# Hybrid layer with experts: the state-space branch product as plain block products between queries and keys, with resident left operands

## The chip, the cores and the metric

The program runs on one core of a Trainium2 chip. The metric is the device time of one execution in microseconds (us); of several runs the median is given. TensorE (PE) multiplies, VectorE (DVE) and ScalarE (ACT) work element by element, GpSimd (POOL) too, and SyncE (SP) issues most of the transfers (DMA), in order.

## The reference, cut to what matters

A layer of two blocks on 1024 tokens with 1024 features, in float32. The change touches only the first block:

```python
h = _rmsnorm(x, pre_g)
proj = jnp.einsum('bld,de->ble', h, w_in)
z_ssm, xbc, dt_raw, q, k, v, f_raw, z_att, g_ssm, g_att = jnp.split(proj, ...)
xbc = jax.nn.silu(_causal_dwconv(xbc, conv_w, conv_b))
...
y_ssm = ...            # y * silu(z_ssm), normed by groups, times a gain
o = _forgetting_attention(heads(q), heads(k), heads(v), log_f)
y_att = o * jax.nn.silu(z_att)
p_ssm = jnp.einsum('ble,ed->bld', y_ssm, w_branch_ssm)
p_att = jnp.einsum('ble,ed->bld', y_att, w_branch_att)
merged = jax.nn.sigmoid(g_ssm) * p_ssm + jax.nn.sigmoid(g_att) * p_att
out = jnp.einsum('bld,de->ble', merged, w_out)
```

## The kernel before

Every large product is made of three matmuls on rounded operands: each float32 operand is split into a high part (rounded, by ACT) and a low part (the rest, by DVE), and PE adds high*high, high*low and low*high.

**The xbc phase** (`phase_dense`, "xbc") multiplies h by the columns of xbc and one half of g_ssm: 5 jobs of 8 steps of 24 matmuls, with the causal convolution (`convolve_xbc`) and the decays (`Decays`) on DVE beside it, 6 taps of the convolution in step 8. `KeptOperands` (L1064) meanwhile writes the operands of the later products of h to DRAM (`h_ops`): the split quarters A11 to A22 in steps 0 to 7 (L1086), and four sums S1 to S4 of each of 4 chunks, which POOL adds (L1127 to L1132), ACT rounds (L1110) and POOL splits (L1141).

**`phase_units`** (L1247) computes z, the other half of g_ssm, the queries, keys and values of the attention, and the branch product of y. A unit is a product of 1024 tokens by 1024 columns. A "full" unit uses Winograd's form of Strassen's scheme: 7 products of half-size blocks (`FULL`), whose left operands A and S come from DRAM and whose right operands are sums of quarters of the weights, made by DVE in place (L1500 to L1506). A "half" unit (512 columns) has 4 plain products (`HALF`). A product takes 4 steps; a step multiplies one left by one right operand of 128 rows in 12 matmuls (L1413 to L1416). There are 39 products, 156 steps: z (steps 0 to 27), half of g_ssm (28 to 43), queries (44 to 71), keys (72 to 99), values (100 to 127), branch product (128 to 155).

Left operands (512 KB, high and low) come to four places `bs_a` (L1322), each free when the step 4 earlier is multiplied. Right operands are rounded by ACT (L1432) and split by DVE (L1511) into three places `bs_b`. When a product ends, ACT evicts it (`take`, L1446) or DVE joins it to an earlier one (`join`, L1524), from PSUM to SBUF. For queries, keys and values ACT and DVE then split the result (`finish`, L1471 and L1535), and SP stores the high and the low part, 1 MB each (L1340, L1341), four such pairs a unit. The order of each engine's work is written out by step: at step n an engine first does the step's own operand, then `take` and `join` of product step n-2, `finish` of n-3, and what `beside` and `aside` hang in. SP at n loads the left operand of n, weights that fall due (`load_later`), stores of the product that ended at n-5, and what `on_queue` gives it.

`GatedTurn` (L1557) multiplies y by silu(z), norms and transposes it into yT, PE's part of it before step 44. The operands of the branch product are made of yT by `MadeOperands` (L1145) at every second step from 48 on: 28 operands (7 of each of 4 chunks), of which POOL adds the sums, ACT rounds (L1183) and DVE splits (L1191) into two places `mo_s`, and which SP stores to `y_ops` (L1199) four steps later. Before rounding into a place ACT waits for that place's store:

```python
            if x >= self.RING:
                act.wait_ge(self.kept[x % self.RING], 16 * (x // self.RING))
```

The branch product is the last unit; POOL multiplies it by the gate (L1369). `on_queue` fetches the first heads of the attention at step 138. `phase_forget_attention` (L1719) follows: PE multiplies heads for the row maxima (L1858), DVE takes them (L2029), PE transposes them (L1878), ACT copies them (L1986), sends them to DRAM and fetches them back as a row (L1991, L1996), and then PE scores (L1896). `tail.stored` (L1241) lets an engine wait for all stores of queries, keys and values.

## Time and profile before

| | us |
|---|---|
| median of 3 runs | 2961.45 (2961.43 to 2963.57) |
| the profiled execution | 2964.42 |
| its span, first to last instruction | 2962.6 |
| `phase_units`, first to last product | 524.73 |
| PE busy, share of the span | 93% |
| mean granted clock of PE | 0.964 of full |

The page gives busy times by engine and the costliest groups; the trace behind it answers for a stretch, a line or a tile. A granted clock of 1.00 is 2.4 GHz, 0.50 is 1.2 GHz. Matmuls are pipelined, so the distance between the starts of two is the cost of one, not the time in which one is busy.

### The profile page before, as it was taken

Reading aid. Unit: us, or ns where it says so; the run is one execution under the profiler, and the core shown is the slowest. Engines: PE = TensorE matmul, PEld = TensorE weight load, DVE = VectorE, ACT = ScalarE, POOL = GpSimd, SP = SyncE. Lnnn points to the kernel's source line nnn. Section 1 sums busy time; section 2 is a strip of 40 time slices with the busy share of each in tenths; the row PEclk is TensorE's granted clock in tenths of the full one; section 3 lists DMA queues with packets and bytes.
Section 4 is the critical chain, followed back from the end, with each engine's and each line's share of the span. In section 5 each row is a group of like instructions: output and inputs, shape, how many; then the busy total and the mean of one; then the engine's idle time right before and its main releaser. Section 6 shows DMA issues by size and latency. Waiting matters only on the chain.

```text
span 2962.6 us, 36347 instructions
## 1 busy us (share of the span) xinstructions
PE 2747.2 (93%) x13166; PEld 2244.2 (76%) x13166; DVE 1984.7 (67%) x2312; ACT 1465.7 (49%) x2232; POOL 618.5 (21%) x458
## 2 busy tenths in 40 slices
PE   7899989877888999999998998899999899999997
PEld 6687978766766777788787886778778788888876
DVE  5876756655545555343643687799773699988886
ACT  4544436433323666434343256733432277777775
POOL 3300500100004777100100000000010034333332
PEclk9999989988998999999999998999999999999999
DMA  7420057699886665213212110011213599999996
GB/s 219 169 78 21 1 205 279 229 336 328 283 291 173 138 148 117 61 50 106 84 49 63 50 43 1 15 43 50 100 39 135 186 379 383 370 366 366 367 355 204
DMA packets 199982, 509.61 MB, mean 172 GB/s; under 512 B 75649, under 2 KB 75777, under 8 KB 175008
## 3 DMA queue, kind: packets, MB, share of 16 engines
q1 hardware_dynamic: 189296, 490.78, 48.6%
q0 software_dynamic: 9216, 16.81, 2.3%
q8 instruction: 89, 1.46, 0.2%
q14 instruction: 53, 0.43, 0.0%
q10 hardware_dynamic: 1328, 0.14, 0.0%
HBM read 433.91 MB, written 90.51 MB: 177 GB/s over the span
## 4 chain that ended last, share of the span: by engine, by line
PE 46%; DMA 17%; DVE 9%; POOL 5%; issue 5%; ACT 4%; SPq 1%; POOLq 0%; DVEq 0%; ACTq 0%; PEldq 0%
DMA ex_raw<-in_w_down_e 8%; PE ps L901 7%; PE ps L902 7%; PE ps L903 7%; POOL fa_pl L1841 5%; PE ps L1413 3%; PE ps L1415 3%; PE ps L1416 3%; DMA y_ops<-mo_s 3%; DVE ex_w L3637 3%; PE ps L3487 2%; DMA ex_raw<-in_w_up_e 2%; ACT ex_w L3572 2%; DMA bs_a<-h_ops 1%; PE ps L3215 1%
## 5 line engine op out<-in xcount | busy, mean ns | idle before, releaser
L3637 DVE TENSOR_TENSOR ex_w<-ex_raw,ex_w 128x2048 fp32r<-128x2048 f32 x190 | 430.6, 2289 | 63.8 <-ACT ex_w L3572 61.5
L3572 ACT ACTIVATE ex_w<-ex_raw 128x2048 fp32r<-128x2048 f32 x190 | 361.8, 1917 | 112.4 <-DMA ex_raw<-in_w_up_e 55.0
L3487 PE MATMUL ps<-ex_w,ex_xT 128*128 128x512 f32 x1536 | 367.3, 395 | 14.5 <-DVE ex_xT L3652 14.4
L3487 PEld LDWEIGHTS ps<-ex_w,ex_xT 128*128 128x128 f32 x1536 | 286.5, 189 | 80.1 <-issue 15.6
L1511 DVE TENSOR_TENSOR bs_b<-arena,bs_b 128x512 fp32r<-128x512 f32 x156 | 116.3, 751 | 153.2 <-ACT bs_b L1432 152.9
L793 DVE SCALAR_TENSOR_TENSOR arena<-arena,small 128x1023 f32<-128x1023 f32 (+9 forms) x168 | 215.4, 1282 | 3.5
L1841 POOL TENSOR_TENSOR fa_pl<-fa_p,fa_ph 128x512 fp32r<-128x512 f32 x192 | 196.3, 1039 | 81.4 <-ACT fa_ph L1979 79.3
L1413 PE MATMUL ps<-bs_a,bs_b 128*128 128x512 f32 x400 | 163.7, 409 | 45.0 <-DVE arena L1524 14.5
L1432 ACT ACTIVATE bs_b<-arena 128x512 fp32r<-128x512 f32 x156 | 96.7, 629 | 197.9 <-PE ps L1416 173.3
L3487 PE MATMUL ps<-ex_w,ex_hT 128*128 128x512 f32 x768 | 182.8, 393 | 0.3 <-issue 0.2
L3487 PEld LDWEIGHTS ps<-ex_w,ex_hT 128*128 128x128 f32 x768 | 141.9, 188 | 29.7 <-issue 0.9
L1415 PE MATMUL ps<-bs_a,bs_b 128*128 128x512 f32 x400 | 161.8, 404 | 0.0
L1416 PE MATMUL ps<-bs_a,bs_b 128*128 128x512 f32 x400 | 160.9, 402 | 0.0
L901 PE MATMUL ps<-gb_t,gb_w 128*128 128x512 f32 x368 | 146.1, 397 | 11.5 <-DVE gb_w L1000 3.7
L2029 DVE TENSOR_REDUCE small<-ps 128x1 f32<-128x512 f32 (+1 forms) x192 | 100.7, 553 | 81.3 <-PE ps L1866 43.3
L1009 DVE TENSOR_TENSOR za_t<-arena,za_t 128x1024 fp32r<-128x1024 f32 x48 | 60.1, 1252 | 141.7 <-ACT za_t L962 141.5
L901 PE MATMUL ps<-za_t,za_w 128*128 128x512 f32 x368 | 144.7, 393 | 5.6 <-DVE za_t L1009 3.3
L2837 POOL TENSOR_TENSOR arena<-arena 128x1024 f32<-128x1024 f32 x3 | 8.6, 2877 | 659.7 <-DVE arena L2792 538.9
L902 PE MATMUL ps<-gb_t,gb_w 128*128 128x512 f32 x368 | 144.8, 393 | 0.0
L903 PE MATMUL ps<-gb_t,gb_w 128*128 128x512 f32 x368 | 144.5, 393 | 0.0
L903 PE MATMUL ps<-za_t,za_w 128*128 128x512 f32 x368 | 143.7, 391 | 0.0
L902 PE MATMUL ps<-za_t,za_w 128*128 128x512 f32 x368 | 143.7, 390 | 0.0
(446 smaller groups left out, 6836.4 us busy)
## 6 DMA issues: line engine op xcount, KB each, us to landing
bs_a<-h_ops SPq DMA_DIRECT2D x128, 512.0 KB, 5.3
ex_raw<-in_w_gate_e SPq DMA_DIRECT2D x64, 1024.0 KB, 13.8
ex_raw<-in_w_up_e SPq DMA_DIRECT2D x64, 1024.0 KB, 13.7
ex_raw<-in_w_down_e SPq DMA_DIRECT2D x64, 1024.0 KB, 14.0
arena<-in_w_in SPq DMA_DIRECT2D x72, 512.0 KB, 3.7
arena<-in_w_in SPq DMA_DIRECT2D x18, 1024.0 KB, 8.2
y_ops<-mo_s SPq DMA_DIRECT2D x28, 512.0 KB, 8.5
bs_a<-y_ops SPq DMA_DIRECT2D x28, 512.0 KB, 3.8
```

The source lines that it names most:

```text
L793: ins = dve.scalar_tensor_tensor(out=acc[:, b, back:], in0=src[:, b, 0:SEQ - back], scalar=w, in1=acc[:, b, back:], op0=ALU.mult, op1=ALU.add)
L901: nc.tensor.matmul(c.ps[:, t, :], a[0], b[0], start=(k == 0), stop=False)
L902: nc.tensor.matmul(c.ps[:, t, :], a[0], b[1], start=False, stop=False)
L903: mm = nc.tensor.matmul(c.ps[:, t, :], a[1], b[0], start=False, stop=(n == last[j]))
L1413: nc.tensor.matmul(to, w[0], moving[0], start=(k == 0 and fresh), stop=False, skip_group_check=True)
L1415: nc.tensor.matmul(to, w[0], moving[1], start=False, stop=False, skip_group_check=True)
L1416: mm = nc.tensor.matmul(to, w[1], moving[0], start=False, stop=closes, skip_group_check=True)
L1511: tt(b_slot[n % NB][:, 1, :], place_of[rows[u][x][1]][:, k, :], b_slot[n % NB][:, 0, :].bitcast(F32), ALU.subtract).then_inc(low, 1)
L1841: nc.gpsimd.tensor_tensor(low[x % 4][:, 0:w], prob[x % 3][:, 0:w], f32(high[x % 4][:, 0:w]), ALU.subtract).then_inc(lowered, 1)
L3487: mm = nc.tensor.matmul(out, l, r, start=(k == 0 and n == 0), stop=(k == kc - 1 and n == 2))
L3572: nc.scalar.activation(half_of(part[m][0], h), raw[m][:, h * W // 2: (h + 1) * W // 2], ACT.Identity).then_inc(high[m], 1)
L3637: V.tensor_tensor(half_of(part[m][1], h), raw[m][:, h * W // 2: (h + 1) * W // 2], half_of(as_f32(part[m][0]), h), ALU.subtract)\
```

## The change

- The branch product is no full unit at the end but two units of a new kind, "here", between queries and keys, each 4 plain products on 512 columns (`HALF`). Their left operands are not fetched: ACT rounds and DVE splits each directly from yT into the place `bs_a`. DVE multiplies the results from PSUM into the gate (`by_dve`). `MadeOperands`, `y_ops` and POOL's products go.
- A11 and A12 for keys and values, and S2 for queries, keys and values, are loaded once and stay (`hold`, `resident`): 2 MB each.
- Four places for right operands (`NB`), and with them `take` and `join` at n-3, `finish` at n-4 (`LAG`).
- The keys go to another region, which later holds the heads; values are the last unit. `tail.stored` is split, so that parts can be waited for.
- The sums and low parts of `KeptOperands` go from POOL to DVE, from steps 4 on to steps 0 to 8; the stores of A11 to A22 go from steps 0 to 7 to steps 8 to 15; `decays.on_vector` comes ahead of the taps.
- The unit phase starts with two operands ahead of B21, the others and B22, B12 later; PSUM banks are swapped accordingly.

The new order of steps: z (0 to 27), half of g_ssm (28 to 43), queries (44 to 71), branch (72 to 103), keys (104 to 131), values (132 to 159).

```diff
 class KeptOperands:
...
+    def on_vector(self, n):
+        V, T = self.nc.vector, self.nc.vector.tensor_tensor
+        for x in self.at_step(n):
+            both = self.both[x % self.RING]
+            V.wait_ge(self.high, x + 1)
+            T(both[:, 1, :], self.sums[x // 4 % 2][x % 4], both[:, 0, :].bitcast(F32), ALU.subtract)\
+                .then_inc(self.low, 1)
+        k, odd = divmod(n, 2)
+        if odd == 0 and k < CH:
...
+            T(s2, s1, a11, ALU.subtract).then_inc(self.summed, 1)
...
-class MadeOperands:
...
-    NA, NB = 4, 3
+    NA, NB = 4, 4
+    LAG = NB - 1
...
+    def resident(n):
+        u, x = products[n // 4]
+        held = units[u].resident
+        return None if held is None or rows[u][x][0] not in held else held[rows[u][x][0]][n % 4]
+
+    ring = [n for n in range(NS) if resident(n) is None]
+    order = {n: r for r, n in enumerate(ring)}
+    streamed = [n for n in ring if not here[products[n // 4][0]]]
...
         def load_operand(n):
+            if n not in landed:
+                return
...
+            r = order[n]
+            if r >= NA:
+                multiplied_by(sp, ring[r - NA])
...
         load_weights(0, "B11")
         load_operand(0)
+        load_operand(1)
         load_weights(0, "B21")
-        for n in range(1, NA):
-            load_operand(n)
-        if full[0]:
-            load_weights(0, "B22")
-            load_weights(0, "B12")
         for n in range(NS + 8):
-            if NA <= n < NS:
+            if 2 <= n < NS:
                 load_operand(n)
+            if n in (NA, NA + 1) and full[0]:
+                load_weights(0, ("B22", "B12")[n - NA])
...
         def round_weights(n):
...
+            if n in split_here:
+                r = order[n]
+                multiplied_by(act, ring[r - NA])
+                nc.scalar.activation(a_slot[r % NA][:, 0, :], units[u].ops(rows[u][x][0], k), ACT.Identity)\
+                    .then_inc(a_high, 1)
...
-        for n in range(NS + 4):
+        for n in range(NS + LAG + 2):
             if n < NS:
                 round_weights(n)
-            if n >= 2 and n - 2 < NS and (n - 2) % 4 == 3:
-                take(n - 2)
...
+            m = n - LAG
+            if 0 <= m < NS and m % 4 == 3:
+                take(m)
+            m = n - LAG - 1
+            if 0 <= m < NS and m % 4 == 3:
+                finish(m)
...
         def low_weights(n):
             (u, x), k = products[n // 4], n % 4
+            if n in split_here:
+                slot = a_slot[order[n] % NA]
+                dve.wait_ge(a_high, split_here.index(n) + 1)
+                tt(slot[:, 1, :], units[u].ops(rows[u][x][0], k), slot[:, 0, :].bitcast(F32), ALU.subtract)\
+                    .then_inc(a_low, 1)
...
         def join(m):
             u, x = products[m // 4]
+            if u in by_dve and x % 2:
+                for t in range(4):
+                    dve.wait_ge(product, 4 * (m // 4) + t + 1)
...
+                    y = units[u].place(x // 2, 0)[:, t, :]
+                    tt(y, y, c.ps[:, bank(u, rows[u][x][2], t), :], ALU.mult).then_inc(gated, 1)
...
-            tail.stored(act)
+            tail.all_stored(act)
...
         def convolve_xbc(n, tapped, by_act, by_vec, moved):
 
+            operands.on_vector(n)
+            decays.on_vector(n)
             for x in range(FIRST_TAP[n], FIRST_TAP[n + 1]):
...
-            MERGE, HEADS_IN = 128, 138
...
+            MERGE, HEADS_A, HEADS_B = 72, 142, 150
+            held_at = {"A11": (4, 0), "A12": (4, 4 * SEQ), "S2": (3, 0)}
...
+                elif n == GatedTurn.TURN + 5:
+                    sp.wait_ge(gated_turn.turned, 2 * TT)
+                    hold(sp, "S2")
+                elif n == MERGE + 12:
+                    tail.stored(sp, 2)
+                    hold(sp, "A11")
+                    hold(sp, "A12")
+                elif n == HEADS_A:
+                    tail.stored(sp, 4)
                     for h in range(2):
                         heads.load_a(sp, att, h)
+                elif n == HEADS_B:
                     heads.load_b(sp, att, 0)
...
+                + [unit("here", rows_of_y, wcol(a["w_branch_ssm"][0], 0, n), True,
+                        by_columns(c.at(2, n * 4096, 4096), CH)) for n in range(2)] + [
+                unit("full", h_ops, wide_of(w_in, C_K), True, by_columns(R(1)), None, 1.0,
+                     heads_at(("kh", "kl")), (staged, by_columns(early_lows)), held),
                 unit("full", h_ops, wide_of(w_in, C_V), False, by_tokens(R(4)), None, 1.0,
-                     values_at, (staged, by_tokens(lows))),
-                unit("full", y_ops, wide_of(a["w_branch_ssm"][0], 0), True, by_columns(R(4)),
-                     other=by_columns(R(2)))],
-                R(0), 5, within, first=1, begin=forget, aside=aside_units, beside=beside_units,
+                     values_at, (staged, by_tokens(lows)), held)],
+                R(0), 5, within, first=0, begin=forget, aside=aside_units, beside=beside_units,
```

## Rows read from the trace of the kernel before

**Rows 1.** The page, busy time of TensorE.
```profile
PE 2747.2 (93%) x13166; PEld 2244.2 (76%) x13166; DVE 1984.7 (67%) x2312; ACT 1465.7 (49%) x2232; POOL 618.5 (21%) x458
```
**Rows 2.** Stretches: length, busy time (instructions) of PE, PEld, DVE, ACT, POOL; clock; DMA.
```profile
388.72:913.45 524.73, 463.12 (x1937) 375.07 (x1937) 290.50 (x422) 205.20 (x406) 50.85 (x37) 0.94 0.80 277
524.52:913.45 388.93, 331.34 (x1345) 266.00 (x1345) 210.74 (x312) 134.11 (x233) 50.85 (x37) 0.93 0.83 287
```
**Rows 3.** The same view: 28 steps without a wait, and a stretch behind a wait.
```profile
428.68:504.83 76.15, 76.15 (x337) 63.06 (x336) 41.32 (x59) 44.21 (x117) 0.00 (x0) 1.00 0.72 251
...
645.14:650.43 5.29, 5.29 (x13) 4.13 (x14) 2.76 (x5) 2.06 (x4) 0.00 (x0) 0.50 0.91 373
```
**Rows 4.** PE's waits from 388 to 914: us in total, times, longest.
```profile
PE ps L1413 <- DMA bs_a<-h_ops: 23.5, 9, 5.1
PE ps L1413 <- DVE arena L1524: 14.5, 2, 7.4
PE ps L1413 <- ACT arena L1446: 13.7, 2, 7.0
```
**Rows 5.** ACT's waits in the same stretch.
```profile
ACT mo_s L1183 <- DMA y_ops<-mo_s: 102.4, 24, 10.6
...
ACT arena L1446 <- DMA att_qk<-bs_low: 5.1, 1, 5.1
```
**Rows 6.** PE's timeline, units of queries and keys: start, us, operation [idle before <-releaser].
```profile
564.99 0.77 PE L1413 MATMUL ps<-bs_a,bs_b 128*128 128x512 f32 x1 [6.76 <-ACT arena L1446]
...
608.21 0.76 PE L1413 MATMUL ps<-bs_a,bs_b 128*128 128x512 f32 x1 [7.13 <-DVE arena L1524]
...
645.14 0.79 PE L1413 MATMUL ps<-bs_a,bs_b 128*128 128x512 f32 x1 [3.61 <-DMA bs_a<-h_ops]
```
**Rows 7.** The same timeline: start of the phase, then the end of the values' unit.
```profile
407.88 0.50 PE L1413 MATMUL ps<-bs_b,bs_a 128*128 128x512 f32 x1 [2.37 <-DMA bs_a<-h_ops]
...
779.68 0.50 PE L1413 MATMUL ps<-bs_b,bs_a 128*128 128x512 f32 x1 [1.00 <-DMA bs_a<-h_ops]
...
814.72 0.50 PE L1413 MATMUL ps<-bs_b,bs_a 128*128 128x512 f32 x1 [2.11 <-DMA bs_a<-h_ops]
...
821.41 0.79 PE L1413 MATMUL ps<-bs_b,bs_a 128*128 128x512 f32 x1 [3.68 <-DMA bs_a<-h_ops]
```
**Rows 8.** SP's timeline there: a store of heads, an operand, weights, operands.
```profile
803.73 0.37 SPq L1340 DMA_DIRECT2D att_vh<-bs_high  x1
...
804.69 1.09 SPq L1322 DMA_DIRECT2D bs_a<-h_ops  x1
805.82 2.77 SPq L1314 DMA_DIRECT2D arena<-in_w_branch_ssm  x2
808.64 2.45 SPq L1322 DMA_DIRECT2D bs_a<-h_ops  x2
```
**Rows 9.** By tile, `mo_s` and `bs_high`: durations in ns, least, median, most; first and last start.
```profile
L1183 ACT ACTIVATE mo_s<-arena x28: 616/632/634, 530.8 to 741.3; 128x512 fp32r<-128x512 f32 x28
L1191 DVE TENSOR_TENSOR mo_s<-arena,mo_s x28: 684/692/1347, 531.5 to 742.0; 128x512 fp32r<-128x512 f32 x28
...
L1535 DVE SCALAR_TENSOR_TENSOR bs_low<-arena,bs_high x48: 682/684/690, 551.4 to 832.1; 128x512 fp32r<-128x512 f32 x48
```
**Rows 10.** Timeline of the xbc phase: decay copy, low parts, and PE behind one.
```profile
84.13 1.22 DVE L415 COPY arena<-ps 128x1024 f32<-128x1024 f32 x1
...
89.92 1.22 DVE L1009 TENSOR_TENSOR xbc_t<-arena,xbc_t 128x1024 fp32r<-128x1024 f32 x1
...
114.95 1.75 DVE L1000 TENSOR_TENSOR xbc_w<-arena,xbc_w 128x512 fp32r<-128x512 f32 x1
...
116.76 0.50 PE L901 MATMUL ps<-xbc_t,xbc_w 128*128 128x512 f32 x1 [3.39 <-DVE xbc_w L1000]
```
**Rows 11.** Timeline of the start of the attention: the shift's copy, the first score.
```profile
923.12 0.27 ACT L1986 ACTIVATE fa_shift<-ps 8x128 fp32r<-8x128 f32 x1 [17.01 <-PE ps L1878]
...
935.94 0.77 PE L1896 MATMUL ps<-fa_a 128*128 128x512 f32 x1 [9.35 <-DMA fa_b<-att_shifts]
```

More of the change, by code:

```diff
@@ L1223 @@
-Unit = namedtuple("Unit", "kind ops w turned place func scale stores other")
+Unit = namedtuple("Unit", "kind ops w turned place func scale stores other resident")
 FULL = (("A11", "B11", 0, True), ("A12", "B21", 1, True), ("S2", "B11", 0, False), ("S3", "B12", 0, False),
@@ L1265, in phase_units @@
     full = [u.kind == "full" for u in units]
+    halves = [u for u in range(len(units)) if not full[u]]
+    by_dve = [u for u in halves if units[u].func is None]
+    here = [u.kind == "here" for u in units]
+    flat = lambda tile: tile.rearrange("p a s -> p (a s)")
+    def resident(n):
[5 more added lines that the diff above has]
+    streamed = [n for n in ring if not here[products[n // 4][0]]]
+    landed = {n: sum(1 for m in streamed if m <= n and order[m] % NA == order[n] % NA) for n in streamed}
+    split_here = [n for n in ring if here[products[n // 4][0]]]
     tap0 = [12 * sum(full[:u]) for u in range(len(units) + 1)]
     join0 = [16 * sum(full[:u]) for u in range(len(units) + 1)]
-    half0 = [8 * (u - sum(full[:u])) for u in range(len(units) + 1)]
+    half0 = {u: 8 * (by_dve.index(u) if u in by_dve else [h for h in halves if h not in by_dve].index(u))
+             for u in halves}
     made0 = [16 * sum(full[:u]) for u in range(len(units) + 1)]
@@ L1284, in phase_units @@
     stepped, product = S("stepped"), S("product")
-    tapped, joined, halved = S("tapped"), S("joined"), S("halved")
+    tapped, joined, halved, gated = S("tapped"), S("joined"), S("halved"), S("gated")
+    a_high, a_low = S("a_high"), S("a_low")
+    cut = lambda u: gated if u in by_dve else halved
     opened, split_high, split_low = S("opened"), S("split_high"), S("split_low")
-    kept, low_kept, multiplied = [S(f"kept{s}") for s in range(2)], S("low_kept"), S("multiplied")
-    muls = 16 * sum(1 for x in units if x.kind == "full" and x.func is None and x.stores is None)
-    tail = UnitTail(product, 4 * len(products), joined, join0[-1], join0[-2] + 8, low, NS, kept, low_kept,
-                    len(splits), multiplied, muls)
+    kept, low_kept = ([S(f"{n}{s}") for s in range(2)] for n in ("kept", "low_kept"))
     def multiplied_by(eng, m):
@@ L1297, in multiplied_by @@
             eng.wait_ge(stepped, 3 * g + k + 1)
+    tail = UnitTail(product, 4 * len(products), joined, join0[-1], join0[-2] + 8, low, NS, kept, low_kept,
+                    len(splits), multiplied_by)
     def weights_of(u, q):
@@ L1361, in _ @@
         if fill is not None:
-            fill(pool)
-        for u, x in enumerate(units):
-            if x.kind == "full" and x.func is None and x.stores is None:
-                for i, (r, s) in enumerate(JOINS.values()):
-                    for t in range(4):
-                        pool.wait_ge(joined, join0[u] + 4 * i + t + 1)
-                        to, by = x.other(r, s)[:, t, :], x.place(r, s)[:, t, :]
-                        nc.gpsimd.tensor_tensor(to, to, by, ALU.mult).then_inc(multiplied, 1)
+            fill(pool, tail)
     @block.tensor
@@ L3797, in _build @@
             start = Start(c, within[0], R(1), R(0), R(2))
-            operands = KeptOperands(c, within[0], start, R(0), R(2), h_ops, hT_kept)
+            operands = KeptOperands(c, within[0], R(0), R(2), h_ops, hT_kept)
             phase_start(c, start, a["pre_norm_g"][0], a["x"][0], within)
@@ L3873, in aside_units, with rows_of_y @@
                 gated_turn.on_vector(n, opened)
-                made.on_vector(n)
+            def rows_of_y(name, k):
+                i, j = (int(x) - 1 for x in name[1:])
+                return T(R(1))[:, CH * j + k, i * BANK:(i + 1) * BANK]
             wide_of = lambda w, a0: cols(w)[:, :, a0:a0 + 2 * BANK]
-            unit = lambda kind, ops, w, turned, place, func=None, scale=1.0, stores=None, other=None: \
-                Unit(kind, ops, w, turned, place, func, scale, stores, other)
+            unit = lambda kind, ops, w, turned, place, func=None, scale=1.0, stores=None, other=None, held=None: \
+                Unit(kind, ops, w, turned, place, func, scale, stores, other, held)
+            late = {"S2": held["S2"]}
             tail = phase_units(c, "bs", [
```

243 lines of the change are left out of this document (84 added, 159 removed).

## The prediction

> **What bounds the kernel now.** I read the page first: TensorE (PE) is busy 93% of the span [rows 1], so what counts of the other engines is where they make PE wait. The table of stretches comes next: the changed phase, `phase_units`, runs from 388.72 to 913.45 us, 524.73 us at a granted clock of 0.94 [rows 2]. How long would it take with no wait? In an undisturbed part of it 337 matmuls, 28 steps of 12 and the next one, start within 76.15 us at clock 1.00 [rows 3]: 2.72 us a step. The phase has 39 products of 4 steps; 156 steps are 424.4 us, so 100 us are waiting. Most of that lies behind the turning of y: from 524.52 on, 112 steps (304.6 us) take 388.93 [rows 2], so 84.3 us are lost there. A wait costs more than itself: after one of 3.6 us, 13 matmuls took 5.29 us at clock 0.50 [rows 3], some 2.3 us over their 3.0.
>
> PE's waits by releaser say what is late: operand transfers, two joins of VectorE (DVE) and two evictions of ScalarE (ACT) [rows 4]. A join that is 7 us late is not a slow instruction. ACT's own waits name the cause: 102.4 us, 24 times, before `mo_s`, for the store of the y operand two places earlier [rows 5]. `MadeOperands` has two places; ACT sits in that wait with its evictions and roundings queued behind it, and DVE waits for ACT. In the unit of the queries PE so waits 6.76 and 7.13 us [rows 6]; the unit of the keys has the other two of the four. At 645.14 a transfer is 3.61 us late [rows 6]; it stands behind stores of heads and of y operands in SP's queue.
>
> **Removed.** The 28 y operands: 28 ACT and 28 DVE instructions, 28 stores and 28 loads of 512 KB, 16 sums and 16 products on GpSimd (POOL). The last y operand is made by step 102, so the rest of the values' unit, which ends with step 127, is my model of a unit without them. There PE waits 1.00 us behind the first store of heads and 2.11 and 3.68 us behind the second [rows 7]. The second is worse because its two transfers (2 MB, from 803.73) are followed by one operand, two weight blocks of 1 MB and only then the next operand [rows 8]. With the slow clock behind them that is about 9 us a unit.
>
> **PE's work.** The branch product goes from 7 block products to two halves of 4: 160 steps, 4 x 2.72 = **+10.9**. Nothing hides that, since PE is the bound.
>
> **Stalls after the turn.** *Queries:* 9 us as in the model (both weight blocks, now the branch's and the keys', are still fetched at step 25 of the unit). S2's 2 MB goes out six steps (16 us) before its use; an operand issued behind 2 MB of stores was in use 10 us later [rows 7, 8]. I allow 1 us. *Branch:* no operand transfers, so the queries' last stores delay nobody. Its 32 left operands are rounded by ACT and split by DVE. By the nearest rows, 0.63 and 0.69 us [rows 9], a step has two of each: 1.3 us on ACT and 1.4 on DVE, against 2.72, with four places each. In its first eight steps (21.8 us) DVE has 16 low parts (11.0) and the queries' last 16 joins and splits (at most 10.9): it just fits, cost 0. *Keys:* 9 us. *Values:* the first 12 steps are resident, so the keys' last stores delay no operand, and ACT's wait for the keys' low parts before its first eviction, 5.1 us for the same wait now [rows 5], fits into the lead of four steps. Then SP issues 12 transfers of the heads and only then the operand of step 144, with a store behind it: 2.5 us. The second store has no weights behind it: 2 us. The sum is 9 + 1 + 9 + 4.5 = 23.5 in place of 84.3: **-60.8**. Bounds: 5 (all transfers hide) and 50 (rival 1).
>
> **Start of the phase.** The second product waited 2.37 us for an operand [rows 7]. Operands now go out before B22 and B12, but SP still awaits the store of the forget sums in the same place: **-2**, between 0 and -4.
>
> The fourth place for right operands and `LAG` 3 instead of 2 change no date: in both a product's eviction stands behind a rounding that waits for an equally old step. PE gets one step more lead: cost 0, between -5 and +5. `GatedTurn` multiplies one step later and places at the same step 46: 0.
>
> **The xbc phase.** 16 sums and 16 low parts go from POOL to DVE: 32 x 0.69 = 22 us more on DVE in nine steps of 5.4 us. But POOL slows DVE now: the low part at 114.95 takes 1.75 us instead of 0.69, and PE waits 3.39 us for it [rows 10]; with the slow clock that is 5 us, which go. PE's first step, too, waits for a DVE that POOL stretches: 1.5 us. The decay copy stands behind six taps until 84.13 while PE idles; it moves ahead of them, but the taps then stand before step 9's low parts (1.22 us [rows 10] and 0.69), so most of that comes back. Against the gain: in steps with four sums DVE has 6 x 0.69 + 1.9 = 6.0 us of work, and ACT waits on a ring of four operand stores, which SP issues only after a later weight split: by my working 1 to 4 us. I take **-4.5**; bounds -9, and +15 (all 22 us exposed, less the stalls that go).
>
> **Start of the attention.** Now the last unit also splits and stores. DVE does four splits of 0.68 us [rows 9] before its first maximum: the shift, copied at 923.12, 9.7 us after the last product [rows 11], is ready at +12.4. ACT must wait for all stores: issued some 4 us after the last product and 8 us under way, they land at +12 too. PE begins to score at 935.94 [rows 11], +22.5 us after the last product: **+2.5**, between 0 and +8. The row at 935.94 shows the 4 KB row of shifts ending a wait of 9.35 us. The Trainium skill (DMA: Bandwidth & Descriptors, on queues, rings and completion order) says that a completion increment lands only after every earlier write of that DMA engine, across its queues. By that rule the small transfer ends behind the 2 MB stored before it, the term would be nearer +8, and the sum 5 us more.
>
> **Sum:** 10.9 - 60.8 - 2 - 4.5 + 2.5 = -53.9. The profiled execution took 2964.4 us (span 2962.6), which gives 2910.5; the median of the runs is 3.0 below the profiled one, hence **2907.5 us**.
>
> **Rivals.**
> 1. *SP's queue was the cause as much as the y operands.* It keeps 12 pairs of stores of 2 MB and gets 6 MB of resident operands; transfers as late as that at 645.14 come back at each of them. For it: most of PE's waits by number are transfers [rows 4]. Against: the worst stood right behind a y store. 50 of the 84.3 us stay: 2934. Chance 0.15.
> 2. *Slower: the branch steps become serial.* If four places don't hide the rounding and splitting of both operands, each of 32 steps costs 2 x 0.63 + 2 x 0.69 = 2.64 us more [rows 9]: +84.5, 2992. It decides from 53.9 / 32 = 1.7 us a step. For: no step of the trace splits both operands with joins beside it. Against: each engine's share is half a step. Chance 0.04.
> 3. *The transfers hide.* With 36 MB less in the queue (28 operands stored, 156 loaded, against 100 and 12 of resident ones) no store delays an operand; 5 us of stalls stay: 2889. Against: the model's stalls had no y store beside them [rows 7]. Chance 0.12.
> 4. *The change doesn't take away what it seems to.* Joins and evictions would be late by the order of ACT's and DVE's own work, and four stalls of 9 us (7 and the slow clock) return: 2943. Against: the end of the values' unit has none. Chance 0.06.
>
> The forecast has the remaining 0.63. **Range:** 2888 to 2936 takes in the bounds of the small terms, rival 3 and two thirds of rival 1; outside lie rivals 2 and 4 and the ends of the rest. A measurement of this kernel can tell some 0.2% (6 us) from no change. Faster 0.94, same 0.02 (a slow branch that just cancels), slower 0.04.
>
> **What would show it.** Right: 160 steps; no wait before `mo_s`; the stretch from the turn's end to the last product near 339 us, its waits named DMA and standing behind the second store of queries and of keys; the first xbc step near 28.6 us; scoring 25 us after the last product. Wrong: branch steps over 3 us with DVE or ACT as releaser (rival 2), waits of 3 to 5 us on `bs_a` behind every store (rival 1), waits of 7 us for joins and evictions (rival 4), or an xbc phase longer than now.

## The result and the profile after

The changed kernel takes 2904.74 us (median of 4 runs, 2903.17 to 2911.79), the kernel before in the same session 2961.44 (2955.55 to 2963.57). The ratio is 0.9815, 95% interval 0.9802 to 0.9829: 51 to 59 us less. The forecast was 2907.5.

The profiled executions have spans of 2962.6 and 2901.1 us, 61.5 apart. Marks in both traces give each stage its part:

| stage (matmul starts) | before | after | difference |
|---|---|---|---|
| up to the last matmul of the xbc phase | 272.37 | 269.51 | -2.9 |
| to the first product of `phase_units` (unchanged code) | 116.35 | 109.49 | -6.9 |
| `phase_units`, first product to the end of the last | 524.73 | 466.69 | -58.0 |
| last product to first score | 22.5 | 22.3 | -0.2 |
| first score to the next phase's first matmul | 264.6 | 265.8 | +1.3 |
| the rest (unchanged code) | 1762.1 | 1767.3 | +5.2 |

So the phase that was changed gave 58.0, and two stretches whose code is the same moved by -6.9 and +5.2, which matters when terms of 2 to 5 us are judged. The profiled execution of the changed kernel lies 1.6 us below its median, that of the kernel before 3.0 above its own, so the spans differ by more (61.5) than the medians (56.7).

The page, and the table of stretches with its columns as in [rows 2]: the whole phase, what follows the turning of y, and a part without a wait.

```profile
PE 2729.9 (94%) x13214; PEld 2232.0 (77%) x13214; DVE 1961.3 (68%) x2336; ACT 1466.0 (51%) x2228; POOL 518.7 (18%) x394
```

```profile
379.00:845.69 466.69, 452.29 (x1985) 371.78 (x1985) 269.55 (x410) 203.28 (x401) 7.27 (x8) 0.98 0.64 227
...
601.00:746.00 145.00, 145.00 (x640) 119.82 (x639) 82.93 (x131) 58.61 (x100) 0.00 (x0) 1.00 0.42 148
```

```profile
511.72:845.69 333.97, 321.98 (x1393) 263.77 (x1393) 189.17 (x300) 131.85 (x227) 7.27 (x8) 0.98 0.61 215
```

PE now has 116 steps after the turn, 315.5 us at 2.72; they take 333.97, so 18.5 us are lost in place of the 84.3 behind [rows 2]. The stretch from 601 to 746 holds most of the branch product and the larger part of the keys: 145 us, PE busy in all of it, at full clock. GpSimd (POOL) went from 50.85 us in this phase to 7.27, and the transfers from 277 to 227 GB/s.

PE's waits in the phase (us in total, times, longest), and below them ScalarE's (ACT):

```profile
PE ps L1350 <- DMA bs_a<-h_ops: 18.2, 8, 4.9
PE ps L1350 <- ACT arena L1565: 1.1, 1, 1.1
```

```profile
ACT bs_b L1374 <- PE ps L1353: 177.1, 88, 7.7
ACT bs_a L1367 <- PE ps L1353: 51.3, 29, 7.8
...
ACT arena L1389 <- DMA att_qk<-bs_low: 2.3, 1, 2.3
```

The late joins and evictions of [rows 4] are gone, and so is `mo_s` [rows 5]. ACT now waits for PE, which is how the waits of an engine look when it has time to spare. What is left is one releaser, an operand's transfer, and 1.1 us at the turn. Of its 18.2 us 4.9 lie ahead of the first product and 1.3 ahead of the turn. PE's timeline says where the others lie:

```profile
580.60 0.50 PE L1350 MATMUL ps<-bs_a,bs_b 128*128 128x512 f32 x1 [0.41 <-DMA bs_a<-h_ops]
587.93 0.80 PE L1350 MATMUL ps<-bs_a,bs_b 128*128 128x512 f32 x1 [4.32 <-DMA bs_a<-h_ops]
...
753.10 0.50 PE L1350 MATMUL ps<-bs_a,bs_b 128*128 128x512 f32 x1 [1.62 <-DMA bs_a<-h_ops]
759.96 0.50 PE L1350 MATMUL ps<-bs_a,bs_b 128*128 128x512 f32 x1 [3.84 <-DMA bs_a<-h_ops]
...
803.88 0.50 PE L1350 MATMUL ps<-bs_b,bs_a 128*128 128x512 f32 x1 [1.22 <-DMA bs_a<-h_ops]
...
837.40 0.50 PE L1350 MATMUL ps<-bs_b,bs_a 128*128 128x512 f32 x1 [0.59 <-DMA bs_a<-h_ops]
```

The first pair stands behind the second store of the queries, the second behind that of the keys. SP's timeline at the first pair is the picture of [rows 8] again: a store of two times 1 MB, one operand, two weight blocks of 1 MB, and then the operand that PE waits for at 587.93.

```profile
570.70 0.37 SPq L1279 DMA_DIRECT2D att_qk<-bs_high  x1
571.11 0.51 SPq L1280 DMA_DIRECT2D att_qk<-bs_low  x1
572.07 0.44 SPq L1259 DMA_DIRECT2D bs_a<-h_ops  x1
572.55 1.22 SPq L1250 DMA_DIRECT2D arena<-in_w_branch_ssm  x1
573.82 1.35 SPq L1250 DMA_DIRECT2D arena<-in_w_in  x1
575.21 1.77 SPq L1259 DMA_DIRECT2D bs_a<-h_ops  x1
```

### The profile page after: what moved, and what is told of

Its sections match the earlier page's. It is cut to its first block, busy times and chain, and to the rows that moved or that the text cites. A ratio compares the mean times of both kernels' runs of the same rounds, so it can differ in the third digit from the quotient of the medians.

```text
span 2901.1 us, 36284 instructions
## 1 busy us (share of the span) xinstructions
PE 2729.9 (94%) x13214; PEld 2232.0 (77%) x13214; DVE 1961.3 (68%) x2336; ACT 1466.0 (51%) x2228; POOL 518.7 (18%) x394
## 4 chain that ended last, share of the span: by engine, by line
PE 52%; DMA 14%; DVE 7%; POOL 5%; issue 4%; ACT 4%; POOLq 0%; SPq 0%; DVEq 0%; ACTq 0%; PEldq 0%
PE ps L901 7%; PE ps L903 7%; PE ps L902 7%; DMA ex_raw<-in_w_up_e 6%; POOL fa_pl L1800 5%; PE ps L1350 5%; PE ps L1353 4%; PE ps L1352 4%; DMA ex_raw<-in_w_down_e 4%; PE ps L3446 4%; DVE ex_w L3596 2%; DMA bs_a<-h_ops 2%; ACT ex_w L3531 2%; PE ps L3174 1%; PE ps L2207 1%
## 5 line engine op out<-in xcount | busy, mean ns | idle before, releaser
L3531 ACT ACTIVATE ex_w<-ex_raw 128x2048 fp32r<-128x2048 f32 x190 | 362.1, 1917 | 112.9 <-DMA ex_raw<-in_w_up_e 65.8
L3446 PEld LDWEIGHTS ps<-ex_w,ex_xT 128*128 128x128 f32 x1536 | 286.8, 189 | 78.5 <-issue 13.3
L1461 DVE TENSOR_TENSOR bs_b<-arena,bs_b 128x512 fp32r<-128x512 f32 x160 | 110.3, 690 | 148.0 <-ACT bs_b L1374 147.7
L1350 PE MATMUL ps<-bs_a,bs_b 128*128 128x512 f32 x352 | 139.5, 396 | 11.3 <-DMA bs_a<-h_ops 10.2
L1928 ACT ACTIVATE fa_p<-ps 128x512 f32<-128x512 f32 x192 | 94.1, 490 | 92.7 <-PE ps L1865 47.2
L1353 PE MATMUL ps<-bs_a,bs_b 128*128 128x512 f32 x352 | 138.6, 394 | 0.0
L1352 PE MATMUL ps<-bs_a,bs_b 128*128 128x512 f32 x352 | 138.5, 393 | 0.0
```

The source lines that it names most:

```text
L1350: nc.tensor.matmul(to, w[0], moving[0], start=(k == 0 and fresh), stop=False, skip_group_check=True)
L1352: nc.tensor.matmul(to, w[0], moving[1], start=False, stop=False, skip_group_check=True)
L1353: mm = nc.tensor.matmul(to, w[1], moving[0], start=False, stop=closes, skip_group_check=True)
L1461: tt(b_slot[n % NB][:, 1, :], place_of[rows[u][x][1]][:, k, :], b_slot[n % NB][:, 0, :].bitcast(F32), ALU.subtract).then_inc(low, 1)
L3446: mm = nc.tensor.matmul(out, l, r, start=(k == 0 and n == 0), stop=(k == kc - 1 and n == 2))
L3531: nc.scalar.activation(half_of(part[m][0], h), raw[m][:, h * W // 2: (h + 1) * W // 2], ACT.Identity).then_inc(high[m], 1)
```

## The experiments

Twelve kernels were run, in three sessions of four, each session with runs of the kernel before on the same chip (medians 2961.86, 2963.10 and 2962.49 us). Ratios are to those. Four or five executions each; intervals are about 0.17 points to either side (5 us), so smaller differences between two kernels are read from the length of the phase in the traces, or left open. That length has a spread too. Three kernels with the same code in the phase (the changed one, the one with the kept h late, the one with the sums on GpSimd) took 466.69, 467.24 and 464.62 us, and four with both edits on the stores and B12 took 450.0 to 452.9. So a difference of under 3 us between two phases says nothing.

### One: the wait for a place, alone

The kernel before, `MadeOperands.sync`:

```
-        x = self.nth(n - 4)
+        x = self.nth(n - 2)
```

> The kernel before, with each operand made of y handed to its store two steps (some 5.4 us) earlier; nothing else is changed. Theory of the prediction: ScalarE's wait for a place of y-operands (mo_s, 24 waits, 102.4 us) is what kept the rounded weights late, so these waits fall below 30 us, the stalls of TensorE after the turn (84.3 us) shrink by 20 to 45 us, and the time is 2916 to 2941 us. Rival (the queue and the transfers are what is short, the y-operands' wait only stands in front of it): the waits of ScalarE go over to TensorE's waits for operands from h_ops, and the time stays within 8 us of 2961.

2939.89 us, ratio 0.9936 (0.9919 to 0.9954). ACT's and PE's waits in the phase (385 to 890 us):

```profile
ACT bs_b L1432 <- PE ps L1416: 241.2, 110, 7.6
ACT mo_s L1183 <- DMA y_ops<-mo_s: 17.8, 7, 4.7
```

```profile
PE ps L1413 <- DMA bs_a<-h_ops: 43.4, 18, 5.6
PE ps L1413 <- DMA bs_a<-y_ops: 6.3, 3, 4.4
PE ps L1413 <- ACT arena L1608: 1.6, 1, 1.6
```

One number in one line takes 85 of the 102 us off ACT's wait, both late joins and both late evictions with it, and 20.1 us off the phase (504.60 in place of 524.73). Of these, 17.8 lie behind the turn (371.13 us in place of 388.93), where the edit acts; the other 2.3 lie ahead of it, in steps that the edit doesn't touch. So the reading of [rows 5] was right, and the wait stood on PE's path, but the stalls shrank by a little less than the 20 us that the theory gave as its least. But the waits for operands from `h_ops` grew from 23.5 us to 43.4: a part of what was taken away had only stood ahead of them. Both theories of this run hold in part.

### Two: the same stores on another queue

The kernel before; SyncE (SP) issues no y operand, ACT does, in `MadeOperands.on_scalar`:

```
+        act, x = self.nc.scalar, self.nth(n - 1)
+        if x is not None:
+            act.wait_ge(self.low, x + 1)
+            act.dma_start(self.ops[...], self.both[...]).then_inc(self.kept[x % self.RING], 16)
```

> The kernel before, with the stores of y's operands issued by ScalarE one step after it made them (some three steps earlier than SyncE did), on ScalarE's own queue; the traffic is the same. Theory one (the place of the store in SyncE's program and the order of its queue were what cost): ScalarE's waits for a place fall as in the run with stores two steps earlier (102.4 to 17.8 us) and TensorE's waits for operands from h_ops fall too, from 43 to below 25 us: 2915 to 2930 us. Theory two (the traffic itself is what is left: 28 stores and 28 loads of 0.5 MB): the time is that of the run with earlier stores, 2940 within 5 us. Rival: issuing and waiting on ScalarE costs what it gives: above 2945 us.

2942.71 us, ratio 0.9936 (0.9915 to 0.9956), the phase 505.24 us.

```profile
PE ps L1414 <- DMA bs_a<-h_ops: 43.5, 16, 5.7
```

```profile
ACT mo_s L1189 <- DMA y_ops<-mo_s: 4.2, 3, 3.4
```

With the stores out of SP's program and off its queue, the wait for a place is down to 4.2 us, and the operands are as late as in run one, to 0.1 us. So the order in SP's program is not what was left; theory two stands. What the two kernels share, and the changed one lacks, are the 28 stores of 512 KB, the 28 loads of them and the branch's weights as a full unit's; that these transfers are what holds the others up is the simplest reading, but their parts were not told apart.

### Three and four: residents, and the fourth place

The changed kernel without residents (the three calls of `hold` and their waits gone, and):

```
-            late = {"S2": held["S2"]}
+            late = held = None
```

> The changed kernel without resident left operands: S2 for the queries, A11, A12 and S2 for keys and values are again loaded step by step into the ring (28 loads of 0.5 MB come back, 3 loads of 2 MB go). Theory: without them the loads of the first three products of keys and values run beside the stores and weight loads of the unit before, and PE's stalls from the queries to the values (some 18 us) grow by 5 to 20 us: 2910 to 2925. Rival: those loads are hidden anyway, and the time stays within 3 us of 2904.7.

2911.66 us, ratio 0.9832 (0.9816 to 0.9848): 6.9 us more by the medians; the phase takes 474.59 us, 7.9 more. The operand waits rise from 18.2 us to

```profile
PE ps L1350 <- DMA bs_a<-h_ops: 24.5, 13, 4.9
```

and the largest new stall is in step 143, the last of the 12 steps of the values' unit that residents had covered:

```profile
800.44 0.80 PE L1350 MATMUL ps<-bs_b,bs_a 128*128 128x512 f32 x1 [4.26 <-DMA bs_a<-h_ops]
```

SP issued that operand at 791.9 us, behind the 12 loads of the first heads (785.83 to 791.5) and ahead of the values' first store. The last store of the keys (768.20) cost only the 0.98 us that PE waited at 770.81, in step 134. So the size was forecast, at its lower end, but the traffic that the operands met was mostly the heads', not that of the unit before. Then the fourth place:

```
-    NA, NB = 4, 4
+    NA, NB = 4, 3
```

> The changed kernel with three places for right operands in place of four, and the take and finish one step earlier with it. Prediction's term: the fourth place is worth nothing (0, from -5 to +5), so 2904.7 within 3 us. Rival: with three places the weights' rounding runs less far ahead, and the stalls behind the queries' and keys' second stores (7.7 and 7.55 us) and at the turn (8.3 us) grow by 5 to 15 us together, so 2910 to 2920.

2909.16 us, ratio 0.9834 (0.9815 to 0.9852); the phase takes 468.74 us, 2.1 more. The medians differ by 4.4 us, within their spread, and 2.1 is within that of the phase. Some 0.5 of it is at the turn: from PE's first transpose to the next product it is 8.8 us in the four kernels with three places and 8.3 in the ten with four. Zero to two is what the place is worth in the phase, not the 5 to 15 of the rival.

### Five and six: what stands behind the second stores

The changed kernel with B12 of the next unit fetched later:

```
-                    if n == free + 2:
+                    if n == free + (7 if q == "B12" else 2):
```

> The changed kernel with the load of the weights' quadrant B12 (1 MB) issued five steps later (seven steps after its last use in place of two), so that it no longer stands beside the second store (2 MB) of queries and keys. Theory: TensorE's waits behind the second stores of queries and keys (7.7 and 7.55 us in the changed kernel) come from the traffic that store and weight loads make together, and a quarter of it less takes 4 to 10 us off: 2895 to 2901 us. Rival: the half-megabyte operand load itself stands behind the store's own 2 MB, and the time stays within 3 us of 2904.7.

and with the low parts stored later:

```
                         sp.dma_start(to_high, staged(u, i).bitcast(F32)).then_inc(kept[i % 2], 16)
+                    elif n == step0[u] + 4 * x + 3 + 7:
+                        to_high, to_low = units[u].stores(r, s)
                         sp.dma_start(to_low, ...).then_inc(low_kept[i % 2], 16)
```

> The changed kernel with the store of each low part (1 MB) issued two steps after that of its high part in place of right behind it. Theory: as in the run before, what is late after the second stores is the operand's load behind 2 MB of stores, and it takes 4 to 12 us off: 2893 to 2901 us. Rival one: the traffic is the same in sum, and the wait only moves two steps on: within 3 us. Rival two: the buffer of low parts comes free later, ScalarE waits longer for it at the first take of the next unit (2.3 us now), and the time grows by 2 to 6 us.

B12 later: 2899.39 us, ratio 0.9788 (0.9772 to 0.9805), the phase 456.90. Low parts later: 2893.33 us, ratio 0.9763 (0.9746 to 0.9780), the phase 456.99. The two stretches, B12 first:

```profile
380.99:837.89 456.90, 448.00 (x1984) 368.93 (x1985) 269.30 (x410) 203.07 (x400) 7.27 (x8) 0.99 0.66 232
```

```profile
380.89:837.88 456.99, 449.94 (x1984) 371.52 (x1985) 269.62 (x410) 203.63 (x401) 7.28 (x8) 0.99 0.66 231
```

Either edit takes 9.8 us off the phase. With the low parts later, two waits are left in place of the four rows from 580.60 to 759.96:

```profile
587.26 0.50 PE L1352 MATMUL ps<-bs_a,bs_b 128*128 128x512 f32 x1 [2.10 <-DMA bs_a<-h_ops]
...
754.49 0.50 PE L1352 MATMUL ps<-bs_a,bs_b 128*128 128x512 f32 x1 [2.09 <-DMA bs_a<-h_ops]
```

Neither rival came: the wait did not move two steps on, it became smaller, with the same bytes spread over two more steps. By the medians, the low parts give more (11.4 us against 5.4, or by the ratios, which take out the session, 15 against 8); their intervals touch, and the phases are equal, so this difference is not settled.

### Seven and eight: the kept h, and all three edits

The changed kernel, in the attention's program for SP (the 4 MB of h are needed only after the attention):

```
-            sp.dma_start(hT, hT_kept).then_inc(h_back, 16)
             for h in range(HEADS):
+                if h == 3:
+                    sp.dma_start(hT, hT_kept).then_inc(h_back, 16)
```

> The changed kernel with the 4 MB load of the kept h (needed only after the attention) issued after the third head's loads in place of at the attention's start. Theory: from the last product to the first score (22.3 us) 10.1 us are the round trip of the shifts through DRAM, and that round trip runs beside the 4 MB; without them it takes 4 to 7 us less, and the time is 2897 to 2902 us, if the collision with later heads costs nothing. Rival: the round trip is mostly latency of two small transfers one behind the other, and the time stays within 3 us of 2904.7.

2918.03 us, ratio 0.9846 (0.9823 to 0.9869): 13.3 us slower by the medians, 9 by the ratios, outside both theories. In the profile the attention, from the last product to the next phase's first matmul, takes 10.8 us more, and 3.9 more are the clock in the state-space stage (below). PE's waits in the attention:

```profile
PE ps L1818 <- DMA fa_a<-att_qk: 9.4, 1, 9.4
PE ps L1856 <- DMA fa_b<-att_shifts: 8.6, 1, 8.6
```

The second row, at the attention's start, should have shrunk from 6.1 us and grew to 8.6, with no 4 MB beside it. What lay beside it instead were the next heads' loads, which SP issued 1.1 us earlier. The 16 DMA engines were about as full without the 4 MB (share 1.22 during the shift's store, 1.35 in the changed kernel). The store took 4.0 us in place of 3.4 and the way back 7.8 in place of 5.9. So taking out the 4 MB alone frees nothing. The first row is new. SP issues the 4 MB in front of the head's loads:

```profile
924.37 0.59 SPq L1775 DMA_DIRECT2D arena<-hT_kept  x1
925.00 0.59 SPq L1660 DMA_DIRECT2D fa_a<-att_qk  x1
```

They take 14.8 us to land, the head's operands come behind them, and PE goes on at 940.94. At the start of the attention the same 14.5 us lie beside a head whose operands are there already. A transfer that is "needed much later" was moved out of a hollow into a full stretch.

> The changed kernel with all three edits of the runs before (B12 five steps later, low parts two steps later, kept h after the third head's loads). Theory: the gains at the second stores overlap in part (together 8 to 14 us of the 15.3), and that at the attention's start (4 to 7 us) adds: 2884 to 2893 us. Rival: transfers only change places, and the time stays within 5 us of 2904.7.

2903.97 us, ratio 0.9805 (0.9788 to 0.9822). The phase took 450.0 us by the marks of the table, the shortest of all, and the attention gave most of the gain back (10.3 us more than in the next run, which leaves the kept h in place): the rival's time, by another way than the rival's.

### Nine to twelve: the best version, and two questions on it

Both edits that helped, the kept h in its place:

> The changed kernel with the low parts stored two steps later and B12 loaded five steps later, and the kept h left where it is. In the run with all three edits the units took 449.8 us from first to last product against 466.5 in the changed kernel, and the later load of the kept h cost some 13 us in the attention. Theory: 2904.7 - 16.7 = 2888 us, from 2884 to 2892. Rival: with the kept h in its old place the attention keeps nothing of it (2893, as with the low parts alone).

2894.47 us (5 runs, 2888.93 to 2897.66), ratio 0.9773 (0.9756 to 0.9790), above the 2892 of the theory. The stretch:

```profile
377.93:829.01 451.08, 445.89 (x1985) 367.93 (x1985) 269.99 (x410) 203.67 (x401) 7.28 (x8) 1.00 0.67 234
```

The phase gave 15.6 us, as forecast from the run before (16.7), and the whole 10.3: the median is that of the low parts alone. It is faster than both kernels, by some 68 and 10 us. Which of the two versions is better isn't settled.

The same kernel with the attention's loads held back:

```
             for h in range(HEADS):
+                if h == 0:
+                    sp.wait_ge(scored, 1)
```

> The kernel with low parts and B12 later, and in the attention SyncE holds the loads of heads 1 and 2 (and the values behind them) until the first score has been made. Theory: the round trip of the first head's shifts (10.1 us from the shift's transpose to the first score) runs behind those loads, and goes down by 2 to 4 us: 2 to 4 us faster than the kernel without. Rival: head 1's operands, issued some 8 us later and beside the 4 MB of the kept h, come late, and it is 3 to 10 us slower.

2895.33 us, ratio 0.9773 (0.9754 to 0.9793), no difference. PE's wait for the shifts is 6.3 us against 6.0. So removing the 4 MB alone didn't shorten the round trip, and removing the loads of heads 1 and 2 alone didn't either. That doesn't show that traffic costs it nothing, since each of the two runs left the other traffic in place (share 1.34 here). Both at once were not taken out. The second head's store in the run with the kept h late met empty DMA engines (share 0.01, against 1.22 at the first head's), and was done in at most 1.4 us in place of 4.0; the run with all three edits shows the same 1.4:

```profile
883.78 0.27 ACTq L1951 DMA_DIRECT2D att_shifts<-fa_shift  x1
...
885.17 0.22 ACTq L1956 DMA_DIRECT2D fa_b<-att_shifts  x1
```

```profile
862.41:866.39 3.98, 3.13 (x9) 1.68 (x8) 2.78 (x6) 0.00 (x0) 0.00 (x0) 0.50 1.22 219
883.78:885.17 1.39, 1.11 (x7) 0.57 (x6) 1.33 (x3) 1.02 (x3) 1.18 (x1) 1.00 0.01 3
```

Last the xbc part, undone in the changed kernel and in the best one: `KeptOperands` as before, `fill` and `start` handed to it, the decays behind the taps.

> The changed kernel with the xbc part undone: the sums of h's operands go back to GpSimd, two steps of raw operands come first again, and the decays go back behind the taps. Theory one: this part alone is worth the 2.9 us by which the last matmul of the xbc phase moved, so 2907.6 us, and the granted clock in the state-space stage is a matter of its own. Theory two: the stretch of some 14 us at half clock in the state-space stage (before: from 295.6 us; not there in the changed kernel) comes back with it, so 2904.7 + 9.7 = 2914.4 us.

> The kernel of the run before this one (low parts and B12 later), with the xbc part undone: sums of h's operands on GpSimd again. If the second stretch at half clock in the state-space stage belongs to the sums on GpSimd (seen in 3 of 3 profiles with them, in 1 of 7 without), it is seen here and not in the kernel beside it, and this one is 6 to 9 us slower. If it falls by chance, the two differ by the xbc part's own 1 to 3 us.

2912.40 us against 2904.74 (ratios 0.9839, interval 0.9822 to 0.9855, and 0.9815), but 2895.07 against 2894.47 (0.9769, interval 0.9752 to 0.9785, and 0.9773). The first pair says 7 us, the second none.

The clock was a surprise of its own. The state-space stage runs the same instructions in all kernels. It begins with some 12 us of transposes at full clock, and then PE waits 4.30 us for DVE. Right behind that wait PE's granted clock is at half (1.2 GHz) for a few microseconds in every profile. In some it falls again soon after, or stays down longer. The rows are the stretch from 292 to 312 us of: before, after, the changed kernel with the sums on GpSimd, the best one with them there, and the one with the kept h late.

```profile
292.00:312.00 20.00, 18.73 (x95) 17.19 (x94) 7.29 (x10) 7.51 (x28) 11.37 (x7) 0.65 0.00 1
```

```profile
292.00:312.00 20.00, 20.00 (x152) 19.08 (x153) 14.01 (x18) 10.06 (x37) 13.19 (x8) 1.00 0.01 2
```

```profile
292.00:312.00 20.00, 19.39 (x112) 18.45 (x111) 8.36 (x11) 9.00 (x32) 12.89 (x7) 0.74 0.00 1
```

```profile
292.00:312.00 20.00, 18.73 (x96) 17.25 (x94) 7.27 (x10) 7.60 (x28) 11.37 (x7) 0.66 0.00 1
```

```profile
292.00:312.00 20.00, 20.00 (x128) 19.25 (x128) 10.47 (x13) 8.61 (x31) 10.38 (x6) 0.81 0.00 1
```

PE is busy in nearly all of it and gets through 95 matmuls or through 152. From the last xbc matmul to the first product it is 109.2 to 109.6 us where the clock comes back at once, and 113.4 to 116.4 where it does not. The latter is so in all five profiles with the sums on GpSimd, and in one of nine with them on VectorE (DVE), that of the kept h. So neither theory stands as it was put: the slow stretch also comes without those sums, and five of five does not look like chance. What lies ahead is the same in all fourteen profiles: the transposes and the wait together last 16.3 us from the last xbc matmul on. That matmul starts at 270.5 to 272.4 us with the sums on GpSimd and at 266.7 to 271.5 without, so the date alone doesn't decide either. And the second pair of medians is equal though its two profiles differ here by 6.8 us. What decides, and how often it happens in executions that are not profiled, stays open.

## Why the prediction was right, and where not

**The time:** 2907.5 forecast, 2904.74 measured, in the likeliest case. The agreement within 3 us is partly luck. The terms gave 53.9 us and the profiled spans differ by 61.5, so by profiles the forecast is 7 us off (2910.5 against 2903.17). The forecast then assumed that the median again lies 3.0 below the profiled execution, and this time it lay 1.6 above it. The mechanism stands on the phase: 51.9 us forecast for it (10.9 - 60.8 - 2), 58.0 measured. Term by term, by the profiles:

| term | forecast | measured |
|---|---|---|
| 4 more steps | +10.9 | +10.9 (145 us of the branch and the keys without a wait) |
| stalls after the turn | -60.8 (84.3 to 23.5) | -65.8 (84.3 to 18.5) |
| start of the phase, up to the turn's end | -2 | -3.1 (135.80 to 132.72); -1.5 on the mean of three profiles with the old start and eleven with the new |
| fourth place, `GatedTurn` | 0 | 0 to -2 (run with three places; already in the rows above), of which 0.5 at the turn |
| xbc phase | -4.5 | -2.9 at its last matmul |
| state-space stage | not in the sum | -6.9, the clock |
| start of the attention | +2.5 | -0.2 |
| attention and the rest | 0 | +6.5 |

**The cause of the stalls** was named rightly but not in full. I put the whole difference down to the y operands in one number. The runs split the 55.0 us behind the turn (388.93 to 333.97): the wait for a place 17.8 (run one), residents 7.2 (run three), the fourth place 1.7 and within the spread (run four; each taken alone, as if they did not touch each other). The remaining 28, or 39 before the four added steps are paid for, go with the y operands' transfers and the branch as a unit of seven products. No run tells those two apart. Rival 4, joins and evictions late by the order of ACT's own work, fell with run one: they went when the store went out two steps earlier. Rival 1 fell in its size: the transfers behind SP's stores are what is left, but 15.5 us of them stand in two places only, and with 2 MB of stores in one piece beside 2 MB of weights, not at every store.

**The model unit** (the end of the values' unit before) carried the forecast: 9 us for a unit's stores were 7.8 for the queries and 7.7 for the keys. The longest wait was 4.32 and 3.84 us, near the 3.68 of [rows 7]; the one ahead of it 0.41 and 1.62 in place of 2.11, and that behind the first store (1.00) never came. What was worked out from it was too large in the values (4.5 forecast, 2.4 measured with the slow clock; the wait of 1.22 us at 803.88, in step 145, stands behind the heads' transfers and the values' first store), and S2's load cost nothing (1 forecast). *Branch:* 0 forecast, 0 measured, at half the engines' load as worked out; rival 2 is out. Rival 3 (5 us of stalls) did not come by itself; with the edits on the stores and B12 the 116 steps behind the turn take 319.05 us (509.96 to 829.01), 3.5 over their 315.5, and that is rival 3's case.

**The xbc phase** is the step of the working that went least well. The stall I priced at 5 us, behind the low part that POOL stretched, did go. In its place step 9 waits for its low part, behind the taps:

```profile
96.90 0.80 PE L901 MATMUL ps<-xbc_t,xbc_w 128*128 128x512 f32 x1 [4.03 <-DVE xbc_w L1000]
```

The prediction had seen that this would give back most of what the earlier decay copy gains, and set another 1 to 4 us for DVE's load and for ACT's wait on the ring. That wait came too: ACT waited 4.7 and 0.6 us for the ring's stores, and PE 2.7 us for ACT's evictions at 78.10. Waits of PE behind the low parts, the evictions and the decays add up to 9.5 us before (3.4, 4.7, 1.4) and 10.3 after (4.8, 2.7, 1.4, 1.4): nothing gained. The start of the phase did gain. PE's first xbc step is at 29.7 to 30.2 us (mean 29.9) in the five profiles with the sums on GpSimd and at 27.8 to 29.6 (mean 28.5) in the nine without: 1.4 us, where the forecast had 1.5. The last matmul is at 271.6 and 268.9 on the mean: 2.7 us for the whole part, and no single pair of profiles could have told, since the nine alone spread over 4.8. The two pairs of medians (7 us and none) agree with that within their intervals.

**The start of the attention:** the splits cost what was forecast: the shift was copied 12.7 us after the last product (12.4 forecast). The rest came out differently: the shift's round trip through DRAM took 9.6 us in place of 12.8.

```profile
858.37 0.27 ACT L1945 ACTIVATE fa_shift<-ps 8x128 fp32r<-8x128 f32 x1 [11.13 <-PE ps L1837]
858.66 0.55 ACTq L1950 DMA_DIRECT2D att_shifts<-fa_shift  x1
862.04 0.22 ACTq L1955 DMA_DIRECT2D fa_b<-att_shifts  x1
...
867.96 0.76 PE L1855 MATMUL ps<-fa_a 128*128 128x512 f32 x1 [6.12 <-DMA fa_b<-att_shifts]
```

The prediction had allowed only lateness here (between 0 and +8). The way back took the same in both kernels (5.9 and 6.0 us); the difference is the store of 4 KB, done 3.4 us after its issue in place of 6.5 (923.42 to 929.95 before). It was done though the 4 MB of h, issued 0.7 us ahead of it, landed 10 us later.

The Trainium skill (DMA: Bandwidth & Descriptors, on queues, rings and completion order) says that a completion increment lands only after every earlier write of the same DMA engine. The term near +8 that the prediction derived from it didn't come, and it could not: ACT waits for all stores (`tail.all_stored`) before it copies the shift. The last store, issued at 849.41, landed 7.7 us later, 1.5 us before the 4 KB went out, so the 2 MB were never beside it. The kernel before has the same wait in the same place. The step was wrong whatever the rule is. Where the 4 MB were issued 6.9 us ahead of such a store (run with the kept h late), it took 7.7 us and was done at 938.90, some 0.3 us before they landed. That fits the rule; it doesn't prove it.

**The cancellation.** Two terms that no step of the sum foresaw, -6.9 and +6.5, took each other out. Neither is a matter of two single executions. The first is the clock in the state-space stage (slow in five of five profiles with the sums on GpSimd, in one of nine without). As to the second, the rest took 1762.1 to 1765.9 us in the three profiles of the kernel before and its variants and 1767.1 to 1772.3 in the eleven of the changed one and its variants. The stretch from the first score on took 263.7 to 264.6 against 265.8 to 268.2 (without the two runs that move the kept h). So both stretches are slower with the change, by some 8 us on the mean together, and no run here says why. The forecast would have been within the range without that cancellation, but 3 us of agreement is no measure of how well the terms were known.

**The signs.** 160 steps and no wait before `mo_s`: both came. From the turn's end to the last product: 334 us against 339. The waits are named DMA and stand behind the second store of queries and of keys. First xbc step 27.9 us against 28.6, first score 22.3 us after the last product against 25.

## What to carry to other kernels

When a wait is taken away, ask what stands second in the same place. Here a store issued two steps earlier gave 18 us of 84, and what followed was the transfers' own lateness, which only less traffic, or traffic elsewhere, took off.

Large stores and loads that one queue's program issues in one step are worth spreading over the steps behind it: two edits of a line or two took 16 us off the phase (10 by the medians). But look where a transfer lands before moving it: 4 MB moved out of a stretch with slack cost some 10 us.

Taking one of two loads away from a slow transfer tests that load only if the other doesn't fill the DMA engines by itself. Look at their share in the stretch before concluding that traffic doesn't matter.

Take a forecast's small terms for what they are. Stretches of unchanged code moved by 5 to 7 us between the two kernels here, more than most of the terms, and the length of one and the same phase by up to 3 us between profiles.

## What the hardware showed beyond that

The granted clock of a stage can differ between kernels that run the same instructions in it: 0.65 to 1.00 over 20 us of the state-space stage, 95 matmuls against 152, worth some 7 us. What PE did just before was the same in both: some 12 us of transposes and a wait of 4.30 us. The slow stretch came in five of five profiles with the sums on GpSimd and in one of nine without; its cause is open. A comparison of two traces has to begin with the clock by stretch, or such a difference is put down to the change.

A large load issued just ahead of a small store need not hold it up. A store of 4 KB was done in 2.9 to 3.9 us in eleven profiles in which a load of 4 MB had been issued 0.04 to 1.1 us ahead of it, and in 4.0 us in the two in which there was no such load but others (share of the DMA engines 1.22). With the 4 MB issued 1.5 us ahead (the kernel before) it took 6.5, with 6.9 us ahead 7.7, and with the engines idle at most 1.4. In these profiles it took longest where the 4 MB had been on their way longest; with one profile each for 1.5 and 6.9 us that is an observation, not a rule.
